# Decoder layer on one core: the stationary operand's high and low parts interleaved word by word

## What is computed

```python
h = _rmsnorm(x, norm_gain)
proj = h @ w_in                      # (256, 4096) @ (4096, 15416)
(m_q, m_k, m_v, m_o, m_z, m_i, m_f, a_q, ck, cv, sk, sv, wk, wv, a_gate, a_z) = split(proj)
h_m = _mlstm(mq, mk, mv, i_pre, f_pre)      # 4 heads, after a causal convolution of m_q and m_k
y_m = norm(sigmoid(m_o) * h_m) * silu(m_z)
o_a = _nsa(a_q, ck, cv, sk, sv, wk, wv, a_gate, ...)   # 16 heads in 4 groups
y_a = o_a * silu(a_z)
x = x + concatenate([y_m, y_a]) @ w_out     # (256, 4096) @ (4096, 4096)
return _rmsnorm(x, final_norm_gain)
```

## Time and profile before

| | |
|---|---|
| three runs, median | 1850.53 us (1848.96 to 1851.79) |
| profiled execution | 1850.26 us |
| its span, first to last instruction | 1848.5 us |
| around the span | 1.8 us |
| granted TensorE clock, mean | 0.997 |
| TensorE matmul busy | 1821.8 us, 99% of the span |
| weight loads busy (beside the matmuls) | 1512.7 us, 82% |
| VectorE, ScalarE busy | 1141.0 us, 62%; 828.9 us, 45% |
| HBM traffic | 345.62 MB by DMA, mean 187 GB/s |

### The profile page before, as it was taken

How to read it: one execution, slowest core, us unless ns; L and a number is a source line. 1 busy time by engine, 2 the same in 40 slices (tenths; PEclk the granted TensorE clock), 3 DMA queues, 4 the chain that set the end, 5 groups by cost and what they waited for, 6 DMA issues and landing times.

```text
span 1848.5 us, 24131 instructions
## 1 busy us (share of the span) xinstructions
PE 1821.8 (99%) x8488; PEld 1512.7 (82%) x8488; DVE 1141.0 (62%) x1461; ACT 828.9 (45%) x1120; POOL 77.2 (4%) x54
## 2 busy tenths in 40 slices
PE   8999999999999999999999999999999999999997
PEld 6878788888888888888888888888888888888886
DVE  5535644468676676876666666756675775445544
ACT  5534444444454444444444444444444544444443
POOL 0000000000101010010000000000000000000000
PEclk9999999999999999999999999999999999999999
DMA  7676555544545454445555556555555567666664
GB/s 272 184 198 210 194 191 187 193 159 153 178 145 177 152 160 162 156 161 177 191 193 188 173 194 193 184 181 193 194 183 180 173 217 237 204 205 204 204 206 173
DMA packets 100266, 345.62 MB, mean 187 GB/s; under 512 B 10932, under 2 KB 16052, under 8 KB 100052
## 3 DMA queue, kind: packets, MB, share of 16 engines
q1 hardware_dynamic: 93448, 332.68, 54.4%
q10 hardware_dynamic: 6736, 11.77, 2.5%
HBM read 337.07 MB, written 7.33 MB: 186 GB/s over the span
## 4 chain that ended last, share of the span: by engine, by line
PE 96%; DMA 1%; DVE 1%; ACT 1%; issue 0%; POOL 0%; ACTq 0%; DVEq 0%; POOLq 0%
PE acc_a L448 15%; PE acc_a L450 15%; PE acc_a L449 15%; PE acc_b L448 15%; PE acc_b L450 14%; PE acc_b L449 14%; PE bank_v L455 1%; DMA w_raw<-in_w_all 1%; PE bank_z L696 1%; DMA toe_dram<-toe_row 1%; ACT w_split L850 1%; PE bank_x L450 1%; PE bank_x L449 1%; PE bank_x L448 0%; PE bank_v L456 0%
## 5 line engine op out<-in xcount | busy, mean ns | idle before, releaser
L1213 DVE TENSOR_TENSOR w_split<-w_raw,w_split 128x1024 fp32r<-128x1024 f32 x620 | 776.9, 1255 | 597.9 <-ACT w_split L850 594.8
L850 ACT ACTIVATE w_split<-w_raw 128x1024 fp32r<-128x1024 f32 x620 | 655.2, 1059 | 847.8 <-PE acc_a L450 415.7
L448 PE MATMUL acc_a<-w_split,lhs_hi 128*128 128x512 f32 x1216 | 483.7, 398 | 1.7 <-DVE lhs_lo L1282 1.7
L448 PE MATMUL acc_b<-w_split,lhs_hi 128*128 128x512 f32 x1216 | 479.5, 394 | 0.9 <-issue 0.9
L450 PE MATMUL acc_a<-w_split,lhs_lo 128*128 128x512 f32 x1216 | 475.1, 391 | 0.0
L449 PE MATMUL acc_a<-w_split,lhs_hi 128*128 128x512 f32 x1216 | 475.0, 391 | 0.0
L450 PE MATMUL acc_b<-w_split,lhs_lo 128*128 128x512 f32 x1216 | 473.7, 390 | 0.0
L449 PE MATMUL acc_b<-w_split,lhs_hi 128*128 128x512 f32 x1216 | 473.5, 389 | 0.0
L450 PEld LDWEIGHTS acc_a<-w_split,lhs_lo 128*128 128x128 f32 x1216 | 229.0, 188 | 48.8
L448 PEld LDWEIGHTS acc_a<-w_split,lhs_hi 128*128 128x128 f32 x1216 | 229.2, 188 | 47.6 <-issue 2.0
L450 PEld LDWEIGHTS acc_b<-w_split,lhs_lo 128*128 128x128 f32 x1216 | 228.3, 188 | 48.3
(11 more groups left out here) (274 smaller groups left out, 927.1 us busy)
## 6 DMA issues: line engine op xcount, KB each, us to landing
w_raw<-in_w_all SPq DMA_DIRECT2D x616, 512.0 KB
wide<-in_x SPq DMA_DIRECT2D x8, 512.0 KB, 9.4
xres<-in_x ACTq DMA_DIRECT2D x8, 512.0 KB, 4.0
out_y<-wide SPq DMA_DIRECT2D x8, 512.0 KB, 3.1
toe_dram<-toe_row ACTq DMA_DIRECT2D x4, 766.0 KB, 10.3
toe<-toe_dram ACTq DMA_DIRECT2D x4, 512.0 KB, 4.6
gain_f<-in_final_norm_gain ACTq DMA_DIRECT2D x1, 2048.0 KB, 12.2
w_raw<-in_w_all SPq DMA_DIRECT2D x4, 224.0 KB
```

Of the source, the lines that this page charges most:

```text
L448: pe.matmul(dst, a[0], b[0], start=start, stop=False)
L850: act.activation(w_hi[:, cols], w_raw[:, cols], ACT.Copy).then_inc(hi_done, 1)
L1213: dve.tensor_tensor(w_lo[:, cols], w_raw[:, cols], w_hi[:, cols].bitcast(F32), ALU.subtract).then_inc(lo_done, 1)
```

## The change

One tensor `lhs` of 64 KiB takes the place of the two. Its innermost order is token, then part: word 2i of a k-tile is the high part of token i, word 2i + 1 its low part. `lhs_hi` and `lhs_lo` are views of it, so no other line of the kernel changes. A load of 128 tokens now reads 128 words that step by 8 bytes, over 1024 bytes, and the writes of `x_hi` and `x_lo`, and the read of `lhs_hi` in `x_lo`, step by 8 bytes too.

The tensor begins right behind `gain_t`, at byte 16640 (65 x 256), which is 256 bytes off a multiple of 512; `gain_mix` moves behind it, and the alignment to 512 bytes falls away. A gap of 128 bytes appears ahead of `w_split`, so that `w_split` and all behind it keep their addresses.

Engine by engine, the built program has the same instructions in the same places (5353 rows on TensorE, 909 on VectorE, 629 on ScalarE, 50 on GpSimd, 76 on SyncE in either); only access patterns and addresses of these operands differ.

```diff
         gain_t = sb("gain_t", KT_IN)
 
+        lhs = sb("lhs", 2 * KT_IN * T, F32R)[:, :].rearrange("p (k t s) -> p s k t", t=T, s=2)
+        lhs_hi, lhs_lo = lhs[:, 0], lhs[:, 1]
         gain_mix = sb("gain_mix", KT_IN)
-        align(4 * P)
-        lhs_hi = sb("lhs_hi", KT_IN * T, F32R)[:, :].rearrange("p (k t) -> p k t", t=T)
-        lhs_lo = sb("lhs_lo", KT_IN * T, F32R)[:, :].rearrange("p (k t) -> p k t", t=T)
         pos_t = sb("pos_t", 2 * CMP_L)
```

## The result

| | before | after |
|---|---|---|
| median | 1850.51 us (1848.96 to 1851.79, 4 runs) | 1891.1 us (1889.24 to 1894.73, 4 runs) |
| span of the profiled execution | 1848.5 us | 1890.6 us |
| granted TensorE clock, mean | 0.997 | 0.998 |
| interval of a wide matmul, all starts from 1600 to 1760 us | 226.67 ns | 233.33 ns |

The changed kernel is **slower**: ratio 1.0219, 95% interval 1.0203 to 1.0235, or +40.6 us by the medians. I had forecast 1802 us. The sign is wrong; the time is inside the stated range, on the side of the slower rival.

A forecast was written before the change was run, and what follows sets the result against it. TensorE was taken as the bound: wide matmuls by their interval of 226.7 ns. From 1850.3 us, -49 for load and stream at one pace and +1 for writes gave 1802 us; 8-in-10 range 1768 to 1932.

The forecast's parts named there:

- slower rival: Wide matmuls: loads touching twice the memory double the loss, interval 240.1 ns, time 1900 to 1948 us; chance 0.31.
- What bounds the kernel: TensorE, 99% busy: time is the number of wide matmuls, 7296, by their interval of 226.7 ns, 1654 us.
- Each wide matmul loses 13.4 ns at the full clock: Wide matmuls: interval 226.7 ns against 213.3 of streaming, a loss absent at half clock; 98 us in all.
- the pot: All wide matmuls: the total loss the change can draw from or add to, 7296 x 13.4 = 98 us.
- The loss depends on how reads of the load fall against reads of the stream: Wide matmuls at full clock: the 13.4 ns come from how the reads meet, not a fixed price of changing weights.
- One load: A weight load of 128 columns stepping by 8 bytes: taken at 188 ns, with 298 for a rival.
- The doubled price: Weight loads: 1.68 ns a column for a 64-byte step against 0.82 adjacent, so up to 298 ns for 128 columns.
- they go at one pace: Wide matmuls: load and stream sweep 1024 and 1008 bytes together, colliding only at the start; interval 220.0 ns, -49 us.
- The rival on the other side: Wide matmuls: each extra read of the stepped load costs the stream, +51 to +98 us, taken at 1930 us; chance 0.31.
- The sign that I had named for it: Profile after: load mean 188 ns with interval above 227 would mean touched lines count, not pace.
- The 256 bytes: Operand's place 256 bytes off a multiple of 512: costed at nothing, left as part of the uncertainty.
- The writes: ScalarE's and VectorE's operand writes at 8-byte steps: mostly under slack, at most 2 us on the path, taken at +1 us.

The follow-up runs named there:

- e7: Kernel before, but each wide matmul streams the first word of its weight block 512 times, leaving out part of the product: 1776.7 us, ratio 0.9605.
- e13: Kernel before, but each wide matmul streams the first 16 bytes of its weight block 128 times, leaving out part of the product: 1774.9 us, ratio 0.9600.
- e12: Kernel before, with the ring of split weights (the stream) moved 16 bytes off a multiple of 2048: 1882.7 us, ratio 1.0154.
- e15: Kernel before, with the ring of split weights (the stream) moved 64 bytes off a multiple of 2048: 1868.2 us, ratio 1.0105.
- e18: Kernel before, with the stationary operand moved to byte 16832, 64 bytes off a multiple of 128, ring unmoved: 1863.7 us, ratio 1.0070.
- e9: Changed kernel, but each wide matmul streams one word 512 times, leaving out part of the product: 1778.0 us, ratio 0.9589 against the kernel before.
- e5: Kernel before, with high and low words of two k-tiles stored in turn, so loads step by 16 bytes: 1938.4 us, ratio 1.0479.
- e4: Kernel before, but each wide load reads one word 128 times, leaving out part of the product: 1877.2 us, ratio 1.0139.
- e10: Kernel before, but all k-tiles except first and last load 16 columns instead of 128, leaving out part of the product: 1866.9 us, ratio 1.0080.
- e6: Kernel before, but all k-tiles except first and last load 64 columns instead of 128, leaving out part of the product: 1863.5 us, ratio 1.0074.
- e2: Kernel before, high and low still apart, but the stationary operand begins at byte 16640, 256 bytes off a multiple of 512: 1850.9 us, ratio 0.9996.
- e8: Kernel before, with the adjacent stationary operand at byte 16772, 4 bytes past a multiple of 16: 1851.3 us, ratio 0.9998.
- e14: Kernel before, but each wide matmul streams the first 64 bytes of its weight block 32 times, leaving out part of the product: 1947.9 us, ratio 1.0536.
- e1: Kernel before with the change's interleaving, but alignment kept, operand beginning at byte 16896: 1889.9 us, ratio 1.0209.
- e16: Changed kernel, with the ring of split weights moved 16 bytes off a multiple of 2048: 1894.4 us, ratio 1.0247 against the kernel before.

## Why the prediction was wrong

**What bounds the kernel.** Right. The time is the number of wide matmuls by their interval, before and after; the regular intervals grew by 42.8 us and the span by 42.1; the rest nets to less than a microsecond.

**"Each wide matmul loses 13.4 ns at the full clock."** Right as a reading, with one split that I couldn't see: 2.5 ns of it are fixed (e7, e13), so the pot was 10.8 ns, 7296 x 10.8 = 79 us, and e7 shows it (-81 us in the regular intervals; -73 us in all, since all other matmuls together take 6 us more there and the intervals of 260 ns and more 2 us). That half clock has no loss held for the 8-byte step as well (0.43 us at a granted clock of 0.50).

**"The loss depends on how reads of the load fall against reads of the stream."** Right, and shown: e12 changes places in memory, no instruction and no pattern, and costs 5 ns, e15 and e18 agree, and e9 against the kernel after shows that the stream has its part.

**One load.** Taken at 188 ns, measured 195, bounds 188 and 298. Right choice, and covered, so without effect on the time beyond 6 ns at an interruption. The doubled price is real at 16 bytes (310 ns, e5), and there it does cost, at the restarts.

**The step that failed: "they go at one pace".** The term was -49 us with ends of -98 and 0, and it measured +43. I had argued from bytes swept: 1024 against 1008 in the same time, so the two would collide at the start and then never again. Nothing in the trace of before showed that load and stream get out of each other's way by having equal paces, and the runs speak against it: a load that stands still (e4) loses 16 ns, an adjacent one 11, one at equal pace 17.5, all against the same stream. More basic than the picture was the fault in the bounds. The term was bounded by 0 above, that is, by today's loss, though I knew of no reason why a new pattern couldn't lose more. The kernel's own rows had the warning: 229 to 230 ns behind an interruption is a loss above today's, from the same kind of load and stream in another phase, and in the compressor a load of another pattern goes with 10 ns over half the columns. All patterns that ran with a stream that takes new lines lie between 226.7 and 241.9 ns: the settled interval of before was the best case among them, and none improved it.

**The rival on the other side.** Its sign was right, its interval of 233 to 240 ns has the measured 233.3 at its lower end, and its lower price, +51 us, is near the +40.6 measured. (Its 1930 us isn't the middle of 1900 to 1948, which is 1924.) Its mechanism was wrong: it let the loss go by the number of the load's reads, and 16 and 64 columns (e10, e6) lose more than 128. The sign that I had named for it, "A load mean of 188 with an interval above 227 would mean that the count of touched lines matters and not the pace", came true but for 7 ns of the load. Its second half holds, and its first is false: one touched line (e4) gives 231.7 ns.

**The 256 bytes** at nothing: right for that distance (e2). Wrong as a rule: 16 bytes cost 32 us (e12).

**The writes** at +1 us: ScalarE +14 ns each, VectorE +1 ns, the first wide matmul 0.06 us later. Under the bound, and nothing on the path.

**What stays open.** Shown is that the loss needs a stream that takes new lines, that it changes with the load's step, its number of columns and its distance from the stream, and that it doesn't exist at half clock. Not shown is the rule that gives its size, nor whether a stream would lose anything with no load beside it. The numbers, 226.7 for 128 adjacent words, 233.3 for 128 at 8 bytes, 230.0 and 227.1 for 64 of either, 241.9 for four lines over and over, follow neither the reads, nor the lines, nor the pace. That both sets of reads are served by the same parts of memory in turn would fit; no run shows what those parts are. Longer runs of one part in turn (two or four words of high, then of low) weren't run. Of the versions that compute the whole layer none beats the kernel before: e2 and e8, adjacent words at a distance of a multiple of 128 bytes to within one word, equal it, and all others are slower.

## What to carry to other kernels

When TensorE streams without a gap at the full clock, compare its interval with columns / 2.4 GHz and with its interval in a stretch at half clock; here 10.8 of 13.4 ns went away with a stream that takes no new lines, and the layout moved the interval between 226.7 and 235.0 ns. A load may run nearly at the full rate by its own duration and still slow the matmul beside it, so cost a new access pattern by the interval, never by the load's row, and give the range room above today's loss unless a reason forbids it. Keep operands of an fp32r product adjacent and keep their alignment to each other when other buffers move: 16 bytes of shift cost 1.5% here.

## What the runs showed of the hardware that I had not expected

- Moving one operand by 16 bytes against the other changes nothing in the instructions or the loads (189 ns), and costs 5 ns on each wide matmul, 32 us in all (e12).
- Loading less is slower: 16 columns give 230.9 ns where 128 give 226.7 (e10).
- A stream over the same 64 bytes costs 241.9 ns, over the same 16 bytes 215.8 (e14, e13).
- The intervals are regular, not noisy. From 1600 to 1760 us all 706 intervals before are 226 or 227 ns, though VectorE, ScalarE and the DMA engines read and write all the while, so it isn't their traffic that sets it. After, they are 229 to 230 and 237 to 238 ns by turns; in e1, 233 or 234; in e16, 231, 237, 234 and 231 to 232. The mean is 233.3 ns in all three.
- A step of 8 bytes costs a load 6 ns, one of 16 bytes 122 ns (e1, e5). Behind an interruption the next interval grows by as much, 6 and 125 ns (the kernel after, e5).
